# First block of a two-block transformer kernel: projection jobs, attention units and modulation pieces in twelve steps, overlapping head tiles, recurrence in pairs

## What is computed

```python
proj = h @ w_in                       # h = rmsnorm(x): 512 x 1024
# hgrn2 (A, 4 heads of 64) and gla (C, 4 heads, key 32, value 64) are both
S_t = diag(f_t) S_{t-1} + k_t v_t^T ; o_t = S_t^T q_t
o_a = head_rmsnorm(o) * silu(g)       # f from a sigmoid with a lower bound
o_c = head_rmsnorm(o) * silu(g)       # log_f = log_sigmoid(g_lr @ w_g_up + b_g) / 16
# rg-lru (B, width 512)
xc = causal_dwconv(xb)                # 4 taps
r, gi = sigmoid(xc @ w_a + b_a), sigmoid(xc @ w_x + b_x)   # block diagonal
a = exp(-8 r softplus(-lam)); h_t = a_t h_{t-1} + sqrt(1 - a_t^2) gi_t xc_t
o_b = h * gelu(gb)
x = x + concat(o_a, o_b, o_c) @ w_out
# second block, computed early because it depends on c alone:
mod = silu(c) @ ada_w + ada_b         # 2 layers x 6 x 1024 columns
```

## Time and profile before

| | us |
|---|---|
| median of 3 runs | 2741.41 (2740.14 to 2744.28) |
| the profiled execution's own time | 2747.93 |
| its span | 2746.2 |
| TensorE busy | 2276.9 (83%) |
| VectorE busy / ScalarE busy | 602.7 / 598.3 |
| first job of the block's w_in starts | 12 |
| first unit (turn of tile 0) starts | 100.41 |
| output projection starts | 334.86 |

### The profile page before, as it was taken

How to read it: one execution, slowest core, us unless ns; L and a number is a source line. 1 busy time by engine, 2 the same in 40 slices (tenths; PEclk the granted TensorE clock), 3 DMA queues, 4 the chain that set the end, 5 groups by cost and what they waited for, 6 DMA issues and landing times. The chain is left out here.

```text
span 2746.2 us, 21764 instructions
## 1 busy us (share of the span) xinstructions
PE 2276.9 (83%) x8350; PEld 1018.2 (37%) x8350; DVE 602.7 (22%) x1345; ACT 598.3 (22%) x980; POOL 161.2 (6%) x258
## 2 busy tenths in 40 slices
PE   8997899999999986766878777499899488878772
PEld 4443444444444444442222222144355322223221
DVE  2233712211002026430010000130373300000103
ACT  2224311000002026311121111120392121111211
POOL 2111102000000000001000000100021100000001
PEclk9997899999999997877988999799999688999996
DMA  7275927512311120027999999911002389999994
GB/s 252 78 264 200 330 105 282 223 39 93 101 61 61 61 123 1 16 81 302 429 426 429 428 428 428 406 32 50 31 1 108 145 339 429 428 428 428 428 428 177
DMA packets 127483, 624.86 MB, mean 228 GB/s; under 512 B 14165, under 2 KB 17629, under 8 KB 102845
## 3 DMA queue, kind: packets, MB, share of 16 engines
q1 hardware_dynamic: 108672, 557.11, 50.2%
q0 software_dynamic: 13488, 49.86, 4.9%
q10 hardware_dynamic: 5260, 17.05, 1.5%
HBM read 571.31 MB, written 52.67 MB: 227 GB/s over the span
## 5 line engine op out<-in xcount | busy, mean ns | idle before, releaser
L1623 PE MATMUL ps<-ring,arena 128*64 128x512 f32 x2048 | 518.6, 668 | 133.2 <-ACT arena L1651 115.5
L218 PE MATMUL ps<-hT,ring 128*128 128x512 f32 (+3 forms) x1456 | 617.0, 586 | 4.2 <-issue 4.2
L218 PEld LDWEIGHTS ps<-hT,ring 128*128 128x128 f32 (+1 forms) x1456 | 273.5, 190 | 346.3 <-issue 343.5
L1623 PEld LDWEIGHTS ps<-ring,arena 128*64 128x64 f32 x2048 | 161.2, 153 | 468.9 <-issue 386.0
L225 PE MATMUL ps<-ring,hT 128*128 128x512 f32 x640 | 284.9, 604 | 3.3 <-ACT hT L186 1.6
L1638 PE MATMUL ps<-ring,arena 128*64 128x512 f32 x1024 | 237.0, 617 | 31.6 <-ACT arena L1658 31.6
L225 PEld LDWEIGHTS ps<-ring,hT 128*128 128x128 f32 x640 | 122.5, 194 | 156.6 <-issue 153.8
L1681 DVE TENSOR_TENSOR arena<-ps,arena 128x512 f32<-128x512 f32 x32 | 22.1, 692 | 605.4 <-PE ps L1623 605.4
L965 PE MATMUL ps<-ring,arena 128*128 128x512 f32 x336 | 144.8, 592 | 0.8 <-issue 0.8
L1638 PEld LDWEIGHTS ps<-ring,arena 128*64 128x64 f32 x1024 | 82.0, 141 | 164.5 <-issue 127.4
L152 ACT ACTIVATE arena<-x 128x1024 f32<-128x1024 f32 x32 | 33.8, 1056 | 315.2 <-DVE x L1025 132.4
(11 more groups left out here) (326 smaller groups left out, 2008.4 us busy)
## 6 DMA issues: line engine op xcount, KB each, us to landing
ring<-in_expert_w_gate SPq DMA_DIRECT2D x64, 2048.0 KB, 17.1
ring<-in_expert_w_down SPq DMA_DIRECT2D x64, 2048.0 KB, 19.7
ring<-in_expert_w_up SPq DMA_DIRECT2D x64, 2048.0 KB, 19.6
ring<-in_ada_w SPq DMA_DIRECT2D x24, 2048.0 KB, 15.0
arena<-token_slots SPq DMA_DIRECT2D x32, 512.0 KB, 22.8
output_slots<-arena ACTq DMA_DIRECT2D x32, 512.0 KB, 10.2
token_slots<-arena POOLq DMA_DIRECT2D x1, 12288.0 KB, 44.6
output_slots<-arena POOLq DMA_DIRECT2D x1, 12288.0 KB, 80.1
```

Of the source, the lines that this page charges most:

```text
L218: mm = pe.matmul(out, w[:, c, cols], x[:, c, :], start=(c == 0), stop=(c == chunks - 1))
L1623: mm = pe.matmul(k.ps[slots, 2 + kind, :], k.xT[:, c, slots], w[:, c, :], start=(c == 0), stop=(c == KD - 1))
```

## The change

`FIRST_JOBS` puts 16, 17 and 18 before the steps. `STEPS` lists twelve pairs: a job and how many units follow it. Each step ends with one modulation piece. Jobs 12 to 15 come last. `GATE_JOB` moves to step 0, C's decay on ScalarE to step 1, B's gates to step 9 and the turn of A's output to step 11. The units of the three tiles form one list (tile 1's turn ahead of tile 0's out). Tile 2's first eight level units come in the steps, and twelve units remain for a12 to a23, one before each. On ScalarE `preps_until` takes the exponentials that the next step's units need. On VectorE the cumulation for tile t+1 is done inside tile t after level 4, its first operand ("kd") after level 6, and the four convolutions inside tile 1 after levels 0, 2, 4 and 6; `recur` is split in `squares` and `recur`, each done for two tiles of B at a time. GpSimd also clears `S_late`, and `gate_gain` of C moves behind tile 2's preparations.

```diff
-EARLY_JOB = 11
-EARLY_ADA = GATE_JOB - EARLY_JOB
-LATE_JOB = ADA_JOB + EARLY_ADA
+FIRST_JOBS = (4, 5, 6, 7, 0, 1, 2, 3, 16, 17, 18)
+STEPS = ((8, 3), (9, 3), (10, 3), (11, 3), (19, 4), (20, 3), (21, 3), (22, 0), (12, 2), (13, 2), (14, 2), (15, 2))
+B_GATE_STEP = 9
+A_TURN_STEP = len(STEPS) - 1
...
-    order = [4, 5, 6, 7, 0, 1, 2, 3] + list(range(8, EARLY_JOB))
-    for n in range(EARLY_ADA):
-        order += [EARLY_JOB + n, ADA_JOB + n]
-    return order + list(range(GATE_JOB, ADA_JOB)) + list(range(LATE_JOB, JOBS_1))
+    order = list(FIRST_JOBS)
+    for n, (j, _) in enumerate(STEPS):
+        order += [j] + ([GATE_JOB] if n == 0 else list(range(B_GATE_JOB, ADA_JOB)) if n == B_GATE_STEP else []) + [ADA_JOB + n]
+    return order + list(range(ADA_JOB + len(STEPS), JOBS_1))
...
+def block_units():
+
+    a, b, c = (tile_units(t) for t in range(3))
+    units = [(0, *u) for u in a[:-1]] + [(1, *b[0]), (0, *a[-1])] + [(1, *u) for u in b[1:]] + [(2, *u) for u in c]
+    return units
+
+
+def preps_for(unit):
+
+    t, kind, i, _ = unit
+    if kind == "level":
+        return PREPS * t + (3 + i if i < N_LEVELS - 2 else PREPS + (t < 2))
+    return PREPS * t + (PREPS + (t < 2) if kind == "out" else 4)
...
+    todo = block_units()
+    for n, (j, count) in enumerate(STEPS):
         w_in_job(j)
-        for u in todo[:2]:
+        if n == A_TURN_STEP:
+            turn_outputs(s.A_normed)
+        for u in todo[:count]:
             unit(*u)
-        todo = todo[2:]
-        modulate(j - EARLY_JOB)
-    for u in todo:
-        unit(*u)
...
+        todo = todo[count:]
+        if n == 0:
+            gate_job()
+        if n == B_GATE_STEP:
+            recurrence_gates()
+        modulate(n)
+    for a in range(len(STEPS), ADA_PIECES):
+        unit(*todo.pop(0))
         modulate(a)
-        for u in todo[:2]:
-            unit(*u)
-        todo = todo[2:]
...
+    units, todo = block_units(), [(t, *it) for t in range(3) for it in items]
+    ends = list(itertools.accumulate(count for _, count in STEPS))
+
+    def preps_until(last):
+        need = max(preps_for(u) for u in units[:last])
+        while todo and 3 * PREPS - len(todo) < need:
             prep(*todo.pop(0))
...
+    empty(18)
+    preps_until(ends[0])
+    for n, (j, _) in enumerate(STEPS):
+        empty(j)
+        preps_until(ends[min(n + 1, len(STEPS) - 1)])
+        if n == 0:
+            empty(GATE_JOB)
+        if n == 1:
+            decay_gate()
+        if n == B_GATE_STEP - 2:
+            head_norm(2, 0)
+        if n == A_TURN_STEP:
+            for f in range(2):
+                act.wait_ge(s.out_turned, f + 1)
+                act.copy(k.oT[:, f, :], k.ps[:, 2 + f, :]).then_inc(s.A_emptied, 1)
+        if n == B_GATE_STEP:
+            for b in range(B_GATE_JOB, ADA_JOB):
+                empty(b)
+        empty(ADA_JOB + n)
+    decays((0, 1))
+    for n, a in enumerate(range(len(STEPS), ADA_PIECES)):
+        for _ in range(1 if n else 2):
+            if todo:
+                prep(*todo.pop(0))
+        empty(ADA_JOB + a)
+        if n == 0:
+            roots((0, 1))
+        if n == 2:
+            for t in range(B_TILES):
+                act.activation(k.gg[:, t, :], k.gg[:, t, :], ACT.Gelu_apprx_tanh).then_inc(s.gelu_ready, 1)
+        if n == 5:
+            decays((2, 3))
+        if n == 8:
+            roots((2, 3))
     head_norm(4, 1)
     for f in range(2):
         act.wait_ge(s.out_turned, 3 + f)
...
-            if t == 2 and i in (2, 4, 5, 7):
-                recur((2, 4, 5, 7).index(i))
-
-    def recur(t):
+            if t < 2 and i == 4:
+                if t:
+                    decay_gate()
+                cumulate(t + 1)
+            if t < 2 and i == 6:
+                prep(t + 1, "kd", 0)
+            if t == 1 and i % 2 == 0:
+                convolve(i // 2)
+            if t == 2 and i in (2, 5):
+                for b in ((0, 1) if i == 2 else (2, 3)):
+                    squares(b)
+            if t == 2 and i in (4, 7):
+                for b in ((0, 1) if i == 4 else (2, 3)):
+                    recur(b)
+
+    def squares(t):
...
+    cumulate(0)
+    prep(0, "kd", 0)
     attend(0)
     attend(1)
     head_norm(0, k.VA, s.A_normed)
...
-    ch.link(dve.memset(k.S_late[:, :, :], 0.0))
+    dve.wait_ge(s.bd_clear, 2)
     attend(2)
     head_norm(1, k.VC, s.C_normed)
...
     pool.wait_ge(s.unit_done, A_UNITS)
     pool.wait_ge(s.prep_ready, 2 * PREPS)
     pool.memset(k.bd[:, :, :, :], 0.0).then_inc(s.bd_clear, 1)
-    pool.wait_ge(s.bd_clear, 1)
+    pool.memset(k.S_late[:, :, :], 0.0).then_inc(s.bd_clear, 1)
+    pool.wait_ge(s.bd_clear, 2)
     for g, w in enumerate((k.rg_w_a, k.rg_w_x)):
         for b in range(2):
             rows = slice(b * HEAD, (b + 1) * HEAD)
             pool.dma_start(k.bd[rows, g, :, rows], w[0].rearrange("(t b) i j -> b i t j", b=2)[b]).then_inc(s.bd_landed, 16)
-    gate_gain(k.VC, k.normw[:, 256:512], GATE_JOB - 1)
     for kind, i in [("kd", 0)] + [("level", i) for i in range(len(LEVELS))]:
         prep(2, kind, i)
 
+    gate_gain(k.VC, k.normw[:, 256:512], GATE_JOB - 1)
```

## The result

The changed kernel takes 2756.81 us (median of five runs, 2755.06 to 2759.12) against 2741.41 us for the kernel before (five runs beside them, 2739.86 to 2746.09): a ratio of 1.0053, 95% interval 1.0038 to 1.0068, so 10 to 19 us slower. Forecast were 2752 us and 11 us. The profiled execution took 2759.12 us, its span is 2757.4 us.

What follows compares the result with a forecast made beforehand. TensorE up to job 15, then the weight ring: 134.8 us work, 30.4 waits and 7 clock end job 15 at 273; 1 + 65.7 + 5.5 start the projection at 345, 10.3 later; with 1 of clock, 2752 us, range 2736 to 2763.

Steps and rivals of the forecast that it cites:

- Work, 134.8 us: TensorE's work from 100.4 us to the end of job 15, without waits: 134.8 us.
- Step 0: TensorE's wait at the first turn shrinks from 3.23 us to the copy of the turn, 0.6 us.
- Third levels: In steps with three levels, the third waits for VectorE's operand: 1.3 us each, 1.4 behind the state, 6.6 us together.
- Step 2: a2 waits for ScalarE, whose exponential of tile 1's kd precedes C's decay and the emptying of a1: 6.1 us.
- Step 3: The out of tile 0 follows level 7 at once and waits for its emptying: 1.1 us.
- Step 6: Tile 2's kd and a convolution precede VectorE's emptying of tile 1's level 7, so the out waits 12 us.
- Step 8: VectorE does A's head norm and tile 2's first operands before copying tile 2's turn: 4 us, between 0 and 5.8.
- Clock, 7 us: TensorE's lower granted clock after three waits of 4 to 12 us: 7 us, between 5 and 10.
- The ring: After job 15, twelve weight pieces take 65.7 us, the first byte 1 and the reload of x 5.5.
- The tail, "both hidden": Behind job 15, TensorE's some 37 us and VectorE's some 40 us of work are hidden below the reads.
- the tail's own chain: Rival: ScalarE stands at the roots, emptyings and exponentials wait, adding up to 10 us: 2762 us; chance 0.07.
- smaller waits: Rival: tail not bound by the ring; job 15 before 257 us, at 250 the time is 2728 us; chance 0.14.

Runs made afterwards that it cites:

- Run 1: Changed kernel with VectorE's kd of tile 2 and last convolution behind level 7 of tile 1, ScalarE's exponential following: 2746.8 us, 1.001 to the kernel before.
- run 4: Changed kernel with ScalarE's exponential of tile 1's kd one step later, after emptying a1: 2750.62 us, one run.
- run 7: Changed kernel with kd, reload and gate moves combined, A's head norm in step 6, tile 2's kd behind it, one exponential more in step 11: 2725.1 us, ratio 0.9921.
- the mended kernel: The changed kernel with all mends together, as in run 7: 2725.1 us, ratio 0.9921 to the kernel before.
- run 2: Changed kernel with the reload of x issued only when the first w_out piece has landed: 2756.29 us, ratio 1.0045 to the kernel before.
- run 6: Changed kernel with B's eight gate jobs moved from ahead of job 15 to behind it: 2747.33 us, ratio 1.0011 to the kernel before.
- run 3: Changed kernel loading only half of the weights of pieces a13 to a23, so part of the modulation is not computed from its weights: 2738.69 us, one run.
- run of 5: Changed kernel with the recurrence's decays, roots, squares and steps done tile by tile again: 2758.15 us, one run.

## Why the prediction was right, and where its steps were off

Job 15 was forecast at 273 and ended at 271.83; the projection at 345 and 344.81. The sum term by term:

- **Work, 134.8 us.** From the turn at 99.58 to 271.83 are 172.25 us. Less 28.5 of waits and 7.0 of clock, 136.7 are left: 1.9 too few in the sum. The gates took 8.7 us for 7.9, and the state of tile 2, twice as wide, 1.5 for 0.9. The waits came out 1.9 us below their 30.4 and the first turn 0.8 earlier, so that job 15 within 1.2 us is in part luck.
- **Step 0:** 0.65 us for 0.6. **Third levels:** 1.27, 1.28, 1.28, 1.25 and 0.94, 6.0 for 6.6. **Step 2:** 5.56 for 6.1. **Step 3:** 0.95 for 1.1. **Step 6:** 12.35 for 12. Each is a chain whose members all had rows before, and each came out within 0.6 us. The two large ones, of steps 6 and 2, were also shown by removal (runs 1 and 4).
- **Step 8:** 2.99 us for 4, the one term taken by feel between 0 and 5.8. Run 1 showed what feeds it: whatever delays A's head norm. With the head norm a step earlier and kd behind it (run 7) it is 0.70 us.
- **Clock, 7 us:** a2 1.7, the out of tile 1 2.3 (203.72 to 208.61 where the mended kernel needs 2.6), a6 1.3, the state 0.75, a8 0.9: 7.0.
- **The ring:** 73.0 us from job 15 to the projection for the 72.2 forecast, by luck: two wrong terms cancel. What comes on top of the bytes is 5.8 us, not the 1 us to the first byte, a term that no row before had shown; the reload of x costs 1.6 to 2.3, not 5.5 (run 2); the pieces take 5.41 us each, not 5.48, as the ring runs at 387 to 389 GB/s. By the 358 GB/s that "DMA: Bandwidth & Descriptors" of the Trainium skill gives (section Specifications) the twelve pieces would take 5 us longer than the 64.9 here (an estimate); the trace has the higher rate and decides.
- **The tail, "both hidden":** right in effect and mis-sized. The engines' chain is 60 us, not about 40, and run 6 shows it as the bound as soon as 7.7 us of work join it. The rival "the tail's own chain" deserved more than 0.07: it would have decided with a job 15 as late as here and a chain 13 us longer. For the same reason the expectation of run 3 failed. (Of tile 2, the steps hold the turn, the state and six level units, not eight level units as the description of the change says; the prediction counted them rightly.)
- **The pairs:** worth nothing, as far as the one run of 5 shows.

The rival "smaller waits" named its point: job 15 before 257 us. Run 7 went through it, 240.33, and gained more than that rival said. So the change's plan, fewer units behind the `w_in` jobs, does work; the order on VectorE and ScalarE around tile 2's kd spent it. In the two profiles the loss is 9.95 us at the projection and 1.3 behind it, 11.2 in all. The medians differ by 15.4. The interval of the ratio (10.4 to 18.6 us) holds both. The kernel before, run again beside the experiments, had medians of 2744.7 to 2744.9 us (13, 15 and 7 runs), some 12 us below the changed kernel's 2756.81, so the 15.4 is probably 3 us too large by the low median of its five runs. The changed kernel itself was not run again, so this isn't shown.

Left open: whether more work can be moved from ahead of job 15 to behind it, since the reads need some 71 us from there and the engines 63.6, and what part of the low clock comes back without the 5 us wait that is left in the tail.

## What to carry to other kernels

In a ring with a strict queue, look for the instruction that releases a slot with the longest queue behind it. Its end, plus the bytes behind it at the burst's rate and some 6 us, dates everything later; move work from ahead of it to behind it until the engines' own chain is as long as the reads. When units of several tiles are overlapped, write out for each wait the full chain across the engines from the last trigger to the instruction waited for: such sums came out within 0.6 us here, while adding one engine's busy time fell short of the chain by a third. Preparing the next tile early is only good behind the work that someone waits for now.

## What the runs showed of the hardware

- Two DMA queues share unevenly. A 2 MB reload on GpSimd's queue took 14.1 us to land beside the full ring, and 13.4 and 13.5 us when it was issued with the next pieces (runs 2 and 7), but it delayed the ring's piece by only 1.6 us (337.81 to 344.81 is 7.0 us where the cadence without it is 5.4). I had expected a full piece's time, 5.5 us.
- Restarting an idle ring costs more than the 1 us forecast: job 15 ends at 271.83, the DMA share is 0.17 from 272 to 274 us and 0.95 only from 274 to 276 us; the first piece, issued at 272.0 us, takes 9.3 us to land, where the pieces later follow each other every 5.4.
